# Latent attention: pooling's division and subtraction on DVE, splits and roots at other steps, two pooled tiles projected among the heads

## The reference, cut to what matters

```python
def pool_mla_mixer(hn, cos, sin, ...):
    z = hn @ w_in
    u, q_lat, kv_lat, k_rope = jnp.split(z, [c1, c2, c3], axis=-1)      # 512, 384, 256, 32 columns
    u = u.reshape(b, s, POOL_GROUPS, POOL_GROUP_DIM)                    # 4 groups of 128
    pooled = causal_multiscale_pool(u)     # per group: sum over the last 2, 4, 8, 16 tokens / min(t, w), minus u
    pool_out = jnp.einsum('bsgc,gcd->bsgd', pooled, w_pool).reshape(b, s, POOL_DIM) * pool_scale
    q = (rms_norm_2(q_lat, q_a_norm) @ w_q_up).reshape(b, s, MLA_HEADS, QK_HEAD_DIM)
    kv = (rms_norm_2(kv_lat, kv_a_norm) @ w_kv_up).reshape(b, s, MLA_HEADS, QK_NOPE_DIM + V_HEAD_DIM)
    ...                                    # k gets the shared rotary part; q and k are normed per head, rotated
    attn = causal_attention(q, k, v).reshape(b, s, MLA_HEADS * V_HEAD_DIM)
    return jnp.concatenate([pool_out, attn], axis=-1) @ w_out
```

## Time and profile before

| | us |
|---|---|
| median of three runs | 2800.9 |
| the profiled execution | 2800.89 |
| its span | 2799.1 |
| PE busy | 2767.0 (99%) |
| DVE busy | 1426.5 (51%) |
| ACT busy | 999.2 (36%) |
| POOL busy | 522.1 (19%) |

### The profile page before, as it was taken

How to read it: one execution, slowest core, us unless ns; L and a number is a source line. 1 busy time by engine, 2 the same in 40 slices (tenths; PEclk the granted TensorE clock), 3 DMA queues, 4 the chain that set the end, 5 groups by cost and what they waited for, 6 DMA issues and landing times.

```text
span 2799.1 us, 33658 instructions
## 1 busy us (share of the span) xinstructions
PE 2767.0 (99%) x12834; PEld 2293.4 (82%) x12834; DVE 1426.5 (51%) x1387; ACT 999.2 (36%) x1086; POOL 522.1 (19%) x368
## 2 busy tenths in 40 slices
PE   8999999999999999999989999999999999999999
PEld 6978789878888888888768888888888888888887
DVE  5778656556654354443476444434443455644422
ACT  3433534434342243432253443324343222243421
POOL 1134104040011220052133100121010321500100
PEclk9999999999999999999999999999999999999999
DMA  4221123322323322233302222322322323222232
GB/s 164 76 76 65 45 104 122 106 76 90 105 90 105 105 90 105 90 105 105 113 31 76 90 94 101 105 102 93 104 91 95 115 90 106 90 95 100 90 105 90
DMA packets 38812, 266.05 MB, mean 95 GB/s; under 512 B 4304, under 2 KB 4688, under 8 KB 7248
## 3 DMA queue, kind: packets, MB, share of 16 engines
q1 hardware_dynamic: 37152, 259.01, 26.9%
q10 hardware_dynamic: 1584, 5.95, 0.6%
HBM read 262.85 MB, written 2.10 MB: 95 GB/s over the span
## 4 chain that ended last, share of the span: by engine, by line
PE 96%; DVE 2%; ACT 1%; issue 0%; DMA 0%; POOL 0%; DVEq 0%; SPq 0%; POOLq 0%; ACTq 0%
PE ps L1734 30%; PE ps L1735 30%; PE ps L1736 30%; PE ps L1890 1%; DVE w_lo L874 1%; PE ps L2003 1%; PE ps L2294 1%; PE ps L1912 1%; PE ps L2268 1%; PE ps L1972 0%; PE ps L2280 0%; PE ps L1986 0%; ACT w_hi L445 0%; DMA stage<-in_stream 0%; PE ps L1774 0%
## 5 line engine op out<-in xcount | busy, mean ns | idle before, releaser
L1734 PE MATMUL ps<-x_hi,w_hi 128*128 128x512 f32 x2400 | 944.7, 394 | 12.4 <-DVE w_lo L949 12.4
L445 ACT ACTIVATE w_hi<-stage 128x2048 fp32r<-128x2048 f32 x241 | 462.2, 1918 | 1354.7 <-PE ps L1736 1353.4
L1735 PE MATMUL ps<-x_lo,w_hi 128*128 128x512 f32 x2400 | 934.7, 389 | 0.0
L1736 PE MATMUL ps<-x_hi,w_lo 128*128 128x512 f32 x2400 | 934.7, 389 | 0.0
L874 DVE TENSOR_TENSOR w_lo<-stage,w_hi 128x2048 fp32r<-128x2048 f32 x241 | 603.9, 2506 | 401.9 <-ACT w_hi L445 401.9
L1734 PEld LDWEIGHTS ps<-x_hi,w_hi 128*128 128x128 f32 x2400 | 451.2, 188 | 108.9 <-DVE x_lo L956 12.4
L1735 PEld LDWEIGHTS ps<-x_lo,w_hi 128*128 128x128 f32 x2400 | 451.2, 188 | 95.7 <-issue 3.8
L1736 PEld LDWEIGHTS ps<-x_hi,w_lo 128*128 128x128 f32 x2400 | 451.0, 188 | 94.1
L1734 PE MATMUL ps<-f_hi,w_hi 128*128 128x512 f32 x880 | 342.7, 389 | 0.0
L1735 PE MATMUL ps<-f_lo,w_hi 128*128 128x512 f32 x880 | 342.3, 389 | 0.0
L1736 PE MATMUL ps<-f_hi,w_lo 128*128 128x512 f32 x880 | 342.3, 389 | 0.0
(11 more groups left out here) (395 smaller groups left out, 2617.5 us busy)
## 6 DMA issues: line engine op xcount, KB each, us to landing
stage<-in_stream SPq DMA_DIRECT2D x242, 1024.0 KB, 4.9
h<-in_x SPq DMA_DIRECT2D x4, 512.0 KB, 7.1
h<-in_x ACTq DMA_DIRECT2D x2, 1024.0 KB, 5.7
out_x<-h SPq DMA_DIRECT2D x8, 256.0 KB, 5.7
stage<-in_stream SPq DMA_DIRECT2D x4, 256.0 KB, 8.3
mem_raw<-in_mem ACTq DMA_DIRECT2D x1, 1024.0 KB, 4.9
cnt<-in_constants ACTq DMA_DIRECT2D x1, 1024.0 KB, 8.0
mask_f<-in_constants ACTq DMA_DIRECT2D x1, 448.0 KB, 3.4
```

Of the source, the lines that this page charges most:

```text
L445: act.activation(w_hi[slot][:, :], stage[slot][:, :], ACT.Copy).then_inc(hi_ready, 1)
L1734: pe.matmul(out_ap, wh, xh, start=first, stop=False)
L1735: pe.matmul(out_ap, wh, xl, start=False, stop=False)
L1736: return pe.matmul(out_ap, wl, xh, start=False, stop=last)
```

## The change

- POOL keeps the four adds; it multiplies only the first 16 columns of each group, by 2, 4, 8 or 16 over the count. DVE then does `win * 0.5^(g+1) - u_p` in one instruction a group, behind `key_normed(1)`, and waits there for POOL (`pool_step` 8). The table of counts is 4 x 16 columns wide, not 4 x 512. POOL's adds wait for the split of mla's second chunk.
- The split of mla's second chunk (`c0 + 6`) is ahead of the key tiles on ACT and DVE. The rounding and the subtraction of latents 0 to 2 follow it, among the first key tiles.
- ACT copies the rotary part of the keys in two halves, with the keys' root between them. On DVE `hd_rlo` is ahead of query copy 8, and the split of mla's third chunk follows query copy 9. `pl_hi` is made after head square 3, `pl_lo` behind query copy 12 and its key.
- PE does tile 6 before the key sums. `query_sums(1)` follows tile 16. Tiles 18 and 19 go to banks 7 and 6: tile 18 follows `scores(1)` and ACT evacuates it; tile 19 follows `turn(0)` and DVE evacuates it. `scores(0)` and `scores(1)` wait for the evacuation of tile 17, `values(0)` for that of tile 19.

```diff
@@ -86,7 +86,7 @@
...
 for _name, _n in [("ident", P), ("ones", P), ("band", 384), ("perm1", P), ("causal", P), ("twice", P), ("sel", 224),
-                  ("rope", S), ("count", 4 * S), ("levels", 7 * P)]:
+                  ("rope", S), ("count", 4 * 16), ("levels", 7 * P)]:
     CCOL[_name] = _at
@@ -237,7 +237,7 @@
...
         win = place("win", hid(36), [P, 7, PAD + S])
-        cnt = place("cnt", TMP, [P, 4, S])
+        cnt = place("cnt", TMP, [P, 4, 16])
         v_mla = place("v_mla", hid(29), [P, BLK, MLA_HEADS * MLA_V])
@@ -739,7 +739,7 @@
...
             act.dma_start(pc2[:, :], const_in[:, CCOL["causal"]:CCOL["causal"] + 2 * P + 224]).then_inc(rope2_landed, 16)
-            act.dma_start(cnt[:, :, :], cc("count", 4 * S).rearrange("p (a n) -> p a n", a=4)).then_inc(rope2_landed, 16)
+            act.dma_start(cnt[:, :, :], cc("count", 4 * 16).rearrange("p (a n) -> p a n", a=4)).then_inc(rope2_landed, 16)
             stat(NS0["down1"])
@@ -765,10 +765,15 @@
...
             split_hi((c0 + 5, 0))
-            for n, i in enumerate((3, 4, 0, 1, 2)):
...
+            def lat_rounded(n, i):
...
+            lat_rounded(0, 3)
+            lat_rounded(1, 4)
+            split_hi((c0 + 6, 0))
             for i in range(4):
@@ -777,18 +782,21 @@
...
                 if i == 1:
-                    split_hi((c0 + 6, 0))
+                    for n in range(3):
+                        lat_rounded(2 + n, n)
             act.wait_ge(kr_sum, 1)
-            act.activation(k_h[MLA_NOPE:P, :, :], free(ps[MLA_NOPE:P, 5, :], 0, [[0, MLA_HEADS], [1, S]]), ACT.Copy).then_inc(kr_copied, 1)
-            act.wait_ge(hd_stat, 2)
-            act.activation(hd_r[:, :], ps[:, 4, :], ACT.Sqrt, bias=pc("eps", 0), scale=1.0 / MLA_QK).then_inc(hd_std, 1)
+            for e in range(2):
+                if e:
+                    act.wait_ge(hd_stat, 2)
+                    act.activation(hd_r[:, :], ps[:, 4, :], ACT.Sqrt, bias=pc("eps", 0), scale=1.0 / MLA_QK).then_inc(hd_std, 1)
+                act.activation(k_h[MLA_NOPE:P, 4 * e:4 * e + 4, :], free(ps[MLA_NOPE:P, 5, :], 0, [[0, 4], [1, S]]), ACT.Copy).then_inc(kr_copied, 1)
             split_hi((c0 + 7, 0))
...
                 head_square(i)
-                if i == 6:
+                if i == 3:
                     for g in range(4):
@@ -820,6 +828,8 @@
...
             exponentials(0)
+            mla_done(act, 18)
+            act.activation(u_p[:, 2, PAD:PAD + S], ps[:, 7, :], ACT.Copy, scale=pc("pool_scale", 2)).then_inc(acc_evac, 1)
             for v in range(MLA_HEADS):
@@ -1402,8 +1412,7 @@
...
             a_in(4, False)
-            for i in range(3):
-                lat_rest(2 + i, i)
+            split_lo((c0 + 6, 0))
@@ -1414,7 +1423,7 @@
...
                     mla_done(dve, i)
-                src = ps[:, (t0 + i) % 4, :]
+                src = ps[:, (t0 + i) % 4 if i < 19 else 6, :]
                 if i < 4:
@@ -1428,32 +1437,38 @@
...
                 if v == 0:
-                    dve.wait_ge(kr_copied, 1)
+                    dve.wait_ge(kr_copied, 2)
                 dve.scalar_tensor_tensor(k_h[:, v, :], k_h[:, v, :], pc("k_head", 0), ps[:, 6 + v % 2, :], ALU.mult, ALU.mult).then_inc(la_norm, 1)
...
                 mla_evac(i)
-                if i == 1:
-                    split_lo((c0 + 6, 0))
+                if i in (1, 2):
+                    for n in range(2 * i - 2, min(2 * i, 3)):
+                        lat_rest(2 + n, n)
             dve.wait_ge(hd_std, 1)
...
             mla_evac(7)
-            split_lo((C0["mla"] + 2, 0))
-            mla_evac(8)
             dve.wait_ge(hd_rstd, 1)
...
             dve.tensor_tensor(hd_rlo[:, :], hd_r[:, :], hd_rhi[:, :].bitcast(F32), ALU.subtract).then_inc(hd_rsplit, 1)
+            mla_evac(8)
             mla_evac(9)
+            split_lo((C0["mla"] + 2, 0))
             for i in range(2, 8):
...
                     key_normed(v)
-                if i == 6:
+                if i == 2:
+                    dve.wait_ge(pool_step, 8)
+                    for g in range(4):
+                        u = u_p[:, g, PAD:PAD + S]
+                        dve.scalar_tensor_tensor(u, win[:, g if g % 2 == 0 else g + 3, PAD:PAD + S], 0.5 ** (g + 1), u, ALU.mult, ALU.subtract).then_inc(pool_step, 1)
+                if i == 4:
                     for g in range(4):
...
                         dve.tensor_tensor(pl_lo[:, g, :], u_p[:, g, PAD:PAD + S], pl_hi[:, g, :].bitcast(F32), ALU.subtract).then_inc(pl_ready, 1)
-            for i in range(16, 20):
-                mla_evac(i)
+            mla_evac(16)
+            mla_evac(17)
             dve.wait_ge(rq_turned, 1)
@@ -1506,6 +1521,8 @@
...
                 turned(v)
+                if v == 0:
+                    mla_evac(19)
                 if 2 <= v < 6:
@@ -1673,6 +1690,7 @@
...
             pool.wait_ge(acc_evac, T0["a_in"] + 10)
+            pool.wait_ge(lo_ready, C0["mla"] + 2)
@@ -1690,13 +1708,8 @@
...
             for g in range(4):
-                b = window(g + 1, slice(g, g + 1))
+                b = window(g + 1, slice(g, g + 1))[:, :, 0:16]
                 pool.tensor_tensor(b, b, cnt[:, g:g + 1, :], ALU.mult).then_inc(pool_step, 1)
-            for g in range(4):
-                b = window(g + 1, slice(g, g + 1))
-                pool.wait_ge(pool_step, 4 + g + 1)
-                u = u_p[:, g:g + 1, PAD:PAD + S]
-                pool.tensor_tensor(u, b, u, ALU.subtract).then_inc(pool_step, 1)
@@ -2185,18 +2198,18 @@
...
                 if m == 0:
-                    pe.wait_ge(kr_copied, 1)
+                    pe.wait_ge(kr_copied, 2)
                 for g in range(4):
...
             x_tiles(4, 4, KT)
-            c, t = C0["mla"], T0["mla"]
...
             def mla_out(i):
+                c, t = C0["mla"], T0["mla"]
                 chunk = c + sum(i > m for m in MLA_LAST)
                 begin(chunk, t + i, 1)
-                bank = (t + i) % 4
+                bank = (t + i) % 4 if i < 18 else 25 - i
                 if i < 4:
@@ -2233,10 +2246,10 @@
...
                 mla_out(i)
-            for i in range(2, 6):
+            for i in range(2, 7):
                 mla_out(i)
             key_sums()
-            for i in range(6, 9):
+            for i in range(7, 9):
                 mla_out(i)
@@ -2244,10 +2257,9 @@
...
                     spread(v)
-            for i in range(16, 20):
-                mla_out(i)
-                if i == 17:
-                    query_sums(1)
+            mla_out(16)
+            query_sums(1)
+            mla_out(17)
             pe.wait_ge(la_norm, MLA_HEADS)
@@ -2260,7 +2272,7 @@
...
                 else:
-                    pe.wait_ge(acc_evac, T0["a_out"] - 1 + e)
+                    pe.wait_ge(acc_evac, T0["a_out"] - 2)
                 for blocks in SCORE_BANKS:
@@ -2287,6 +2299,8 @@
...
                     pe.wait_ge(la_ot, v)
+                else:
+                    pe.wait_ge(acc_evac, T0["a_out"])
                 for n in range(BLK):
@@ -2311,8 +2325,12 @@
...
             scores(1)
+            mla_out(18)
             for v in range(MLA_HEADS):
                 turn(v)
+                if v == 0:
+                    pe.wait_ge(hd_rstd, 2)
+                    mla_out(19)
                 if v >= 3 and v % 2:
@@ -2508,9 +2526,9 @@
...
     put("rope", np.concatenate([np.ones((MLA_NOPE, S)), cos, cos, -sin, sin]))
-    count = np.stack([1.0 / np.minimum(np.arange(1, S + 1), 2 << g) for g in range(4)])
+    count = np.stack([(2 << g) / np.minimum(np.arange(1, 17), 2 << g) for g in range(4)])
     put("levels", _level_masks().reshape(P, -1))
-    put("count", np.broadcast_to(count.reshape(1, -1), (P, 4 * S)))
+    put("count", np.broadcast_to(count.reshape(1, -1), (P, 4 * 16)))
     return c
```

## The result

The change made the kernel slower by a little: 2805.97 us (median of 20 runs, 2804.54 to 2806.61) against 2801.47 before (20 runs, 2799.95 to 2802.53), a ratio of 1.0015 with a 95% interval of 1.0008 to 1.0022. The forecast was 2801.4, the range ended at 2803.8. The profiled run of the changed kernel took 2804.71, its span is 2802.9.

What follows compares the result with a forecast made beforehand. PE was busy 2767 of 2799.1 us, so only its pauses could move the time. New pauses 6.95, old ones gone 5.1, tiles -1.5, restarts +0.3 gave +0.55, taken as +0.5: 2801.4 us, range 2798.0 to 2803.8.

Steps and rivals of the forecast that it cites:

- step 2: `lat_lo` subtractions after key copies 1 and 2: waits for POOL's adds delay tile 6 by +2.0, tile 7 by +0.8.
- second rival: At the `lat_lo` subtractions POOL's second add gets in between two: +2.2, 2803.6 us, slower than before; chance 15%.
- Step 1: Split of mla's second chunk ahead of the key tiles: PE's tile 4 starts later, +0.4 us.
- Step 3: Rotated key copied in halves, `hd_rlo` earlier: the pause of 1.45 before the first spread is gone.
- Step 4: Split of mla's third chunk ahead of query copy 10: +0.6 before head 2's spread, +0.2 for head 3.
- Step 5: Pooling's division and subtraction: POOL's part hidden; DVE's four fused instructions, 2.64, delay head 4's spread by +1.45.
- Step 6: `pl_lo` after head 4's key: key 5 late, +0.85; the pause of 1.63 before the first pooled tile gone.
- Step 7: Pooled tiles 18 and 19 in pauses among the heads: -1.5; transposes +0.2, first scores +0.45.
- Step 8: The counts' transfer shrinks from 1024 to 32 KB, long before anyone waits for it: nothing.
- first rival: DVE and POOL don't exclude each other at the three subtractions, tiles 6 and 7 don't pause: near 2798.5; 14%.
- full gain: No new pause, all four old ones gone and the tiles hidden: 6.6 us less, 2794.3; chance 4%.

Runs made afterwards that it cites:

- e10: The kernel before with one more small POOL add (128x512, result unused) ahead of its first windowed add; 2809.04 us against 2801.41.
- e7: The changed kernel with its three `lat_lo` subtractions in a row right behind the split, ahead of key copy 0; 2802.15 us.
- e2: The changed kernel with 18 more matmuls (result unused) on PE filling the pause ahead of tile 6; 2803.77 us, ratio 1.0009.
- e8: e5 with the split of mla's third chunk moved behind normed keys 0 and 1; 2796.75 us, ratio 0.9984.
- e5: e1 with DVE's four fused pooling instructions moved behind normed keys 2 and 3; 2797.67 us, ratio 0.9987.
- e6: e5 with `pl_lo` put back behind head 6's key, as in the kernel before; 2798.72 us, ratio 0.9990.
- e4: The kernel before with only the moves of pooled tiles 18 and 19 among the heads and of `query_sums(1)`; 2800.26 us, ratio 0.9996.
- e11: e8 with `pl_lo` in two pairs, groups 0 and 1 ahead of query copy 12, 2 and 3 behind head 4's key; 2795.58 us, ratio 0.9980.
- e1: The changed kernel with POOL's four adds waiting until all five `lat_lo` subtractions are done; 2798.46 us, ratio 0.9990.
- e3: The kernel before with one edit: POOL's adds wait for the split of mla's second chunk; 2802.07 us, ratio 1.0003.
- e9: The changed kernel with all three `lat_lo` subtractions in a row behind key copy 1, POOL's first add already running; 2807.45 us.

## Why the prediction was wrong

The step that failed is **step 2**, in the sentence "the second, back to back, at 1411.7": I let the two subtractions run in a row and put POOL's second add behind them. I took this from the one row of three at 1404.52, where POOL stayed out. e10 shows that this row proves nothing for an add that is queued behind another. The row that spoke for the second rival, POOL's sum at 1341.60, was such a case: it stood right behind a POOL product that ended at 1341.51. The trace thus had both cases before anything ran. The second rival described what happened, and its place for tile 6, 1415.0, or 13.4 after the first key tile, stands against 13.76 measured. (Its +2.2, though, is 0.5 more than its own places give: tile 7 at 1417.35 for 1415.65 is +1.7.) I gave it 15% and held against it that the code was the same; on DVE it was, on POOL the add was the first in one and the second in the other. Whether that, or that the subtraction had been held, let the add in stays open, as said under e10. The sentence of the Trainium skill (page "SBUF — State Buffer", section "Who interferes with whom") that issue order decides who blocks fits the queued adds of this stage, not the fresh ones of before and of e7: two subtractions that started after the add at 1404.75 went ahead of it. Nor does it fit the queued product at 18.96. I had weighed it against one row only.

The second failure is a term that no case had: **the clock**. I read the granted clock as full in the earlier trace rows and took it as given, while the forecast (2.0) and the second rival (over 4) both had a pause longer than any in the earlier trace rows. With this term the second rival would have been 2803.6 + 1.6 = 2805.2, against 2805.97 measured.

The sum itself has slips of 0.1, too small to matter: its terms as written, 6.95 - 5.1 - 1.5 + 0.3, give +0.65 and not +0.55, and the old pause of 0.97 was taken without the step's share that the others got.

The account against the forecast, from the first key tile to the first spread: tile 6 +2.9 (13.76 for 10.88); the lower clock +1.6 (e2); the pause of 0.8 before tile 7 did not come, since DVE's copy 3 was done at 1416.9 while PE, slow, came to tile 7 only at 1418.9. That makes +3.7, and the first spread came at 25.52 where the forecast had 21.6, +3.9. From there on forecast and trace run in parallel: +3.9 at the first scores.

Point by point:
- Step 1 (+0.4 for tile 4): 5.98 for 5.58, right.
- Step 2: the first subtraction 3.50 behind the first add, right; the second, wrong; the third took 1.78, behind POOL's third add and not its second.
- Step 3 (no pause before the first spread): right, and with room.
- Step 4 (+0.6 and +0.2): a bracket of 0.71 (0.87 by steps), with a second spread later by 0.1; right. e8 shows that it is the split.
- Step 5 (+1.45; POOL hidden): a bracket of 0.96, 1.1 by steps, and e5 gives 1.17 for the move. The mechanism is right, the size was 0.3 too large: the four fused instructions took a step of 2.41 (1430.92 to 1433.33) for my 2.64, and the second spread, head 3's, came to PE 0.1 later than the first. POOL's four small products took 0.93, close to the low end.
- Step 6 (+0.85, and the 1.63 gone): 0.69 by the bracket, 0.85 by steps. Right; e6 gives +0.90 for the way back.
- Step 7 (-1.5 + 0.65 = -0.85): e4 gives -0.76.
- Step 8: nothing seen, not tried alone.
- The first rival (no exclusion) fell with the first subtraction of 3.50. Nearest to the full gain comes e11, -5.7 us in the medians, 1.3 above the price I gave it (2794.3). That is by other means than the change's, and with pauses of 0.34 and 0.21 left.

With the place of POOL's adds alone put right (e1) the stage is 2.13 shorter than before. Of the other parts not all paid: against a place one step later, pooling on DVE costs 1.17 where the change has it (e5), and the third split 0.78 (e8). What it is worth to have pooling's division and subtraction on DVE at all, instead of on POOL, was not tried alone.

## What to carry to other kernels

Where DVE instructions with two SBUF inputs stand near a chain of POOL instructions that read SBUF, price each of them at a full POOL instruction, row or no row, since what lets POOL in is not known; start the chain where DVE works from PSUM. An edit that turns several short waits of PE into one long one can cost the wait plus the matmuls at the lower clock behind it (e3), so look at the longest pause of a schedule and not only at their sum.

## What the runs showed of the hardware

- A DVE subtraction with both inputs in SBUF and a POOL add held each other whole, and the wait is inside the instruction's own time: 3.50, 3.23 and 2.37 in e9 for three of 0.68; 5.12 and 5.09 in before and e7 for an add that takes 3.60 in e1.
- Which of the two goes first is open. In this stage queued adds got in between back-to-back subtractions (changed kernel, e9, e10) and fresh ones waited for the whole row (three subtractions in 1.89 and 1.88). The rows at 18.96 and 892.06 of before go the other way round.
- The granted clock fell 0.4 to 0.7 us behind the end of pauses of 2.09 (e3), 2.10 (e7) and 4.81 (changed kernel), and already within those of 7.08 (e9) and 6.63 (e10), where the first matmul behind takes 0.77 in place of 0.47. It did not fall behind those of 1.45 and 1.63 in before. The fall was worth 1.6 us in e2 and in e3, each.
- Left open: why POOL's first add took 3.90 in the changed kernel, e2 and e9, and 3.60 in e1 and e3, with only copies from PSUM beside it for its first microsecond.
